# Norms of a two-block transformer kernel: sums of squares in token layout, root and reciprocal on 128 by 4, spread over partitions by products with the identity

## What is computed

```python
def rmsnorm(x, g, eps=1e-6):
    return x * rsqrt(mean(x * x, axis=-1, keepdims=True) + eps) * g

for layer in range(2):                                    # first block
    h = rmsnorm(x, g_attn) * (1 + scale1) + shift1        # norm 0, norm 2
    x = x + gate1 * mixer_layer(h, w_in, w_out, ...)
    h = rmsnorm(x, g_mlp) * (1 + scale2) + shift2         # norm 1, norm 3
    u, g = split(h @ w_up)
    x = x + gate2 * ((silu(conv(g)) * u) @ w_down)
x = rmsnorm(x, g_final)

h = rmsnorm(x, ln1)                                       # second block, norm 4
y_rnn, y_att = recurrent_group(h @ w_in), chunk_band_attention(h @ w_in)
mixed = concat([rmsnorm(y_rnn, gn_rnn), rmsnorm(y_att, gn_att)])    # the two group norms, 512 features each
x = x + mixed @ w_out
x = x + memory_cross_attention(rmsnorm(x, ln2), ...)
x = x + hierarchical_moe(rmsnorm(x, ln3), ...)
out = rmsnorm(x, final_norm)
```

## Time and profile before

| | us |
|---|---|
| median of 3 runs | 2549.05 (2545.45 to 2552.98) |
| the profiled execution | 2549.13 |
| its span in the trace | 2547.3 |
| PE busy | 2326.3 (91% of the span) |
| DVE busy | 1171.3 (46%) |
| ACT busy | 870.0 (34%) |

### The profile page before, as it was taken

The page is one execution under the profiler, slowest core; times in us unless marked ns, Lnnn a source line. Parts: engine busy times, 40 slices in busy tenths (PEclk is TensorE's granted clock), DMA queues, the critical chain, the costliest instruction groups (busy, mean ns, idle before and its releaser), DMA issues.

```text
span 2547.3 us, 33126 instructions
## 1 busy us (share of the span) xinstructions
PE 2326.3 (91%) x11912; PEld 1613.7 (63%) x11912; DVE 1171.3 (46%) x2263; ACT 870.0 (34%) x1607; POOL 80.9 (3%) x84
## 2 busy tenths in 40 slices
PE   5999989999998999989999999979989689888886
PEld 3777567888886775568888867847866333333332
DVE  4435755534535345646535435764442432323334
ACT  3323753322324224724313334463442121212222
POOL 0000000000000000000000000000000111111110
PEclk7999799999999996999999999989999799999998
DMA  8563035323332751033233222202413699999996
GB/s 267 173 183 108 1 110 156 96 78 107 93 90 72 207 167 38 2 100 83 100 91 99 91 84 67 91 26 66 149 50 148 231 396 399 410 408 403 411 391 264
DMA packets 251789, 414.43 MB, mean 163 GB/s; under 512 B 21447, under 2 KB 226897, under 8 KB 239185
## 3 DMA queue, kind: packets, MB, share of 16 engines
q1 hardware_dynamic: 235649, 398.25, 44.7%
q0 software_dynamic: 11520, 8.43, 1.0%
q10 hardware_dynamic: 4432, 5.24, 0.6%
HBM read 420.24 MB, written 25.17 MB: 175 GB/s over the span
## 4 chain that ended last, share of the span: by engine, by line
PE 77%; DMA 8%; DVE 7%; issue 4%; ACT 3%; SPq 1%; ACTq 0%; DVEq 0%; PEldq 0%; POOLq 0%; PEld 0%
PE bank L724 9%; PE bank L726 9%; PE bank L725 9%; DMA arena<-in_expert_up_w 7%; PE bank L652 6%; PE bank L654 6%; PE bank L653 6%; PE bank L1104 5%; PE bank L1105 3%; PE bank L1113 3%; PE bank L771 2%; PE bank L745 2%; PE bank L761 2%; PE bank L632 2%; PE bank L679 2%
## 5 line engine op out<-in xcount | busy, mean ns | idle before, releaser
L652 PE MATMUL bank<-hT_r,arena_r 128*128 128x512 f32 x704 | 296.1, 421 | 33.4 <-DVE arena_r L1667 21.2
L1104 PE MATMUL bank<-arena,xT 128*64 128x512 f32 x560 | 262.9, 626 | 49.8 <-DMA arena<-in_expert_up_w 35.9
L654 PE MATMUL bank<-hT_r,arena_r 128*128 128x512 f32 x704 | 278.1, 395 | 0.0
L726 PE MATMUL bank<-hT_r,arena_r 128*128 128x512 f32 x704 | 275.3, 391 | 0.0
L1105 PE MATMUL bank<-arena,xT 128*64 128x512 f32 x560 | 263.3, 627 | 0.0
L653 PE MATMUL bank<-arena_r 128*128 128x512 f32 x656 | 259.2, 395 | 0.0
L725 PE MATMUL bank<-arena_r,S_r 128*128 128x512 f32 x528 | 206.9, 392 | 0.0
L2224 DVE TENSOR_TENSOR hT<-hT,bank 64x512 f32<-64x512 f32 x80 | 54.8, 685 | 319.1 <-PE bank L1092 292.7
L1104 PEld LDWEIGHTS bank<-arena,xT 128*64 128x64 f32 x560 | 78.6, 144 | 166.7 <-issue 148.8
L652 PEld LDWEIGHTS bank<-hT_r,arena_r 128*128 128x128 f32 x704 | 134.5, 191 | 74.6 <-ACT hT_r L1239 22.0
L654 PEld LDWEIGHTS bank<-hT_r,arena_r 128*128 128x128 f32 x704 | 134.1, 191 | 29.3
(11 more groups left out here) (432 smaller groups left out, 4475.8 us busy)
## 6 DMA issues: line engine op xcount, KB each, us to landing
arena<-in_expert_gate_w SPq DMA_DIRECT2D x32, 2048.0 KB
arena<-in_expert_up_w SPq DMA_DIRECT2D x32, 2048.0 KB, 20.4
arena<-in_expert_down_w SPq DMA_DIRECT2D x32, 2048.0 KB, 14.0
arena<-in_w_up SPq DMA_DIRECT2D x88, 512.0 KB, 5.0
arena<-in_w_in SPq DMA_DIRECT2D x68, 512.0 KB, 6.1
arena<-in_w_down SPq DMA_DIRECT2D x40, 512.0 KB, 4.1
arena<-in_w_mod SPq DMA_DIRECT2D x16, 1024.0 KB, 10.0
S<-in_w_mod SPq DMA_DIRECT2D x32, 512.0 KB, 4.6
```

Source lines behind the costliest of these rows:

```text
L652: mm(b[:, :], w_h, hT_r[:, k, :], start=start, stop=False)
L654: return mm(b[:, :], w_l, hT_r[:, k, :], start=False, stop=stop)
L726: return mm(b[:, :], w_slot(arena_r, i, piece)[:, at:at + P], hi, start=False, stop=stop)
L1104: mm(bank[half][gate0:gate0 + SUB, :], x, expert_weights(slot, 0)[:, k, :], start=k == 0, stop=k == KD - 1)
```

## The change

The product is turned round: the tile of squares becomes the stationary operand, 128 tokens at a time, and a column of 1/1024 (or 1/512) the moving one, so that four products per tile of squares leave one mean per token, on 128 partitions by 4 columns. Root and reciprocal work on 128x4. A new step `spread` then makes the 128x512 table again: for each of the 4 columns the reciprocal root, broadcast along 128 columns, is the weight matrix, and the identity is the moving operand. DVE's gain products read the result straight from bank 7 (group norms: banks 4 and 5). It is done for norms 0 to 4 and the two group norms.

```diff
+        mean_of = sb("mean_of", [P, 2, NT])
+        norm_std, norm_root = small[:, 32:36], small[:, 36:40]
...
+            def token_sums(b, k, n, which):
+                for t in reversed(range(NT)):
+                    opens = k == 0 and t == NT - 1
+                    out, of = (bank[b][:, 0:NT], mean_of[:, which, :]) if opens else (bank[b][:, t:t + 1], mean_of[:, which, NT - 1:NT])
+                    ins = mm(out, sq[:, k % 2, t * P:(t + 1) * P], of, start=opens, stop=k == n - 1 and t == 0)
+                ins.then_inc(s["sq_used"], 1)
+
+            def spread(n, b):
+                pe.wait_ge(s["rs_ready"], n + 1)
+                for t in range(NT):
+                    ins = mm(bank[b][:, t * P:(t + 1) * P], norm_root[:, t:t + 1].to_broadcast([P, P]), ident, start=True, stop=True)
+                ins.then_inc(s["root_spread"], 1)
...
                 with pe.If(l > 0):
                     norm(2 * l, b=0)
+                spread(2 * l, 7)
...
                 norm(2 * l + 1, KD - 2)
+                spread(2 * l + 1, 7)
                 with pe.If(l < DEPTH - 1):
                     mod_next(l, MOD_FIRST - 1)
...
             norm(2 * L, b=0)
+            spread(2 * L, 7)
             pe.wait_ge(s["mem_scaled"], 2)
...
                 for k in range(CT):
                     pe.wait_ge(s["sq_ready"], 6 * KD + CT * grp + k + 1)
-                    mm(bank[7][:, :], onesR, sq[:, k % 2, :], start=k == 0, stop=k == CT - 1).then_inc(s["sq_used"], 1)
+                    token_sums(7, k, CT, 1)
+                spread(2 * L + 1 + grp, 4 + grp)
...
-                af(std[:, :], bank[7][:, :], ACT.Sqrt, bias=epsc[:, 0:1]).then_inc(s["std_ready"], 1)
+                af(norm_std, bank[7][:, 0:NT], ACT.Sqrt, bias=epsc[:, 0:1]).then_inc(s["std_ready"], 1)
...
+            def token_root(n, stds):
+                dve.wait_ge(s["std_ready"], stds)
+                vec.reciprocal(norm_root, norm_std).then_inc(s["rs_ready"], 1)
...
+                dve.wait_ge(s["root_spread"], n + 1)
-                        stt(hn[:, k % 2, :], xT[:, k, :], table[:, g + k:g + k + 1], rs[:, :], ALU.mult, ALU.mult).then_inc(s["hn_ready"], 1)
+                    stt(hn[:, k % 2, :], xT[:, k, :], pc[:, g + k:g + k + 1], bank[7][:, :], ALU.mult, ALU.mult).then_inc(s["hn_ready"], 1)
```

More of the change, by code:

```diff
@@ L139 @@
 FIN_AT = 13
-CH_NORM, CH_ROPE, CH_MLP = 1, 2, 2
+CH_ROPE, CH_MLP = 2, 2
 MLP_SLOTS = 2 * (UP_SLOTS + DOWN_SLOTS)
@@ L1221, in _, with norm_sum @@
             af(cz[:, :, 0:1].rearrange("p k o -> p (k o)"), small[:, 8:8 + KD], ACT.Silu).then_inc(s["silu_c"], 1)
-            def norm_sum(n, before, b=7, also=None):
+            def norm_sum(n, before, b=7, also=None, by_token=True):
                 for k in range(KD):
@@ L1232, in norm_sum @@
                 act.wait_ge(s["sq_used"], n * KD + KD)
-                af(std[:, :], bank[b][:, :], ACT.Sqrt, bias=epsc[:, 0:1]).then_inc(s["std_ready"], 1)
+                root, of = (norm_std, bank[b][:, 0:NT]) if by_token else (std[:, :], bank[b][:, :])
+                af(root, of, ACT.Sqrt, bias=epsc[:, 0:1]).then_inc(s["std_ready"], 1)
             def norm_shift(n, shift):
@@ L1326, in _ @@
             act.wait_ge(s["lam2_abs"], 1)
-            af(small[:, 40:44], small[:, 40:44], ACT.Exp, scale=-1.0).then_inc(s["lam2_exp"], 1)
+            af(small[:, 40:44], small[:, 40:44], ACT.Exp, scale=-1.0).then_inc(s["lam_exp"], 1)
             for c in range(MOD_FIRST):
@@ L1438, in _ @@
             act.wait_ge(s["sq_used"], 2 * L * KD + KD)
-            af(std[:, :], bank[0][:, :], ACT.Sqrt, bias=epsc[:, 2:3]).then_inc(s["std_ready"], 1)
+            af(norm_std, bank[0][:, 0:NT], ACT.Sqrt, bias=epsc[:, 2:3]).then_inc(s["std_ready"], 1)
             for k in range(KD):
@@ L1523, in beside_out2 @@
                     af(mem_hi[:, 2 * k - 2:2 * k, :], mem_full[:, 2 * k - 2:2 * k, :], ACT.Copy).then_inc(s["mem_ready"], 1)
-            norm_sum(7, 64, also=beside_out2)
+            norm_sum(7, 64, also=beside_out2, by_token=False)
             proj_split2(IN2 + OUT2 + 1)
@@ L1689, in _ @@
             vec.memset(one6[:, :], 1.0)
+            link(vec.memset(mean_of[:, :, :], 0.0))
+            for which, width in enumerate((D, D_RNN)):
+                vec.memset(mean_of[:, which, NT - 1:NT], 1.0 / width)
             vec.memset(gpad[:, :, :], 0.0)
@@ L1744, in norm_recip, with norm @@
                 link(vec.reciprocal(rs[:, :], std[:, :]))
-            def norm(n, g, table, shift, stds=None, out=hT, done="h_ready", halfway=False):
-                if not halfway:
-                    norm_recip(n if stds is None else stds)
+            def norm(n, g, shift):
+                dve.wait_ge(s["root_spread"], n + 1)
                 for k in range(KD):
[L1751 to L1754, removed]
-                        stt(hn[:, k % 2, :], xT[:, k, :], table[:, g + k:g + k + 1], rs[:, :], ALU.mult, ALU.mult).then_inc(s["hn_ready"], 1)
[L1756 to L1761, removed]
+                    if k >= 2:
+                        dve.wait_ge(s["h_ready"], n * KD + (k - 1))
+                        dve.wait_ge(s["h_lo_ready"], n * KD + (k - 1))
+                    stt(hn[:, k % 2, :], xT[:, k, :], pc[:, g + k:g + k + 1], bank[7][:, :], ALU.mult, ALU.mult).then_inc(s["hn_ready"], 1)
+                    if k >= 1:
+                        shift_rest(n, k - 1, shift)
+                shift_rest(n, KD - 1, shift)
             def shift_rest(n, k, shift):
@@ L1766, in shift_rest, with norm_split @@
                 stt(h_lo[:, k, :], hn[:, k % 2, :], pc[:, shift + k:shift + k + 1], hT_r[:, k, :], ALU.add, ALU.subtract).then_inc(s["h_lo_ready"], 1)
-            def norm_split(done, g, also=None):
+            def norm_split(done, g, root, also=None):
                 for k in range(KD):
@@ L1923, in _ @@
                         split_lo(l, 0)
-                norm(2 * l + 1, C_GM, pc, SH2)
+                token_root(2 * l + 1, 2 * l + 2)
+                norm(2 * l + 1, C_GM, SH2)
                 with dve.If(l < DEPTH - 1):
@@ L2030, in _ @@
             for grp, g in enumerate((E_GR, E_GA)):
-                dve.wait_ge(s["std_ready"], 7 + grp)
-                link(vec.reciprocal(rs[:, :], std[:, :]))
+                token_root(2 * L + 1 + grp, 7 + grp)
+                dve.wait_ge(s["root_spread"], 2 * L + 2 + grp)
                 src = (xc, o2)[grp]
```

39 lines of the change are left out of this document (20 added, 19 removed).

## The result

The changed kernel takes 2561.11 us (median of 8 runs, 2555.67 to 2566.83) against 2549.59 of the kernel before on the same chip (8 runs): a ratio of 1.0042, 95% interval 1.0032 to 1.0052, 11.5 us slower. Its profiled execution took 2561.64 us, with a span of 2559.8, 12.5 longer than before.

A forecast was written before the change was run, and what follows sets the result against it. PE's program was taken to bound the kernel (77% of the span). Terms 3.7 + 2.8 + 0 - 1.6 + 5.7 + 5.3 gave +15.9 us on the profiled 2549.13, so 2565 us, range 2543 to 2576.

The forecast's parts named there:

- Prices: Per operation: 64 records of sums 10.5 us (6.9 to 14.1), a spread 1.0 or 1.9, DVE's gain product unchanged.
- Rival 1: All new sums run at PE's upper clock level: -5.8 us, about -12 at best, time 2540; chance 0.17.
- Norm 0, +3.7: Sums and 48 modulation records end at 35.7 against 32.0, later work already at lower clock: 3.7 us slower.
- Norm 1, +2.8: Modulation chunk and folds now start behind the spread: first MLP product at 418.6, not 415.86, 2.8 us slower.
- Norm 2, 0: Sums of 10.5 us, then 2.55 to the gain product, at 795.25: no change (-4 to +4).
- Norm 3, -1.6: Three sums as before, then 2.55 us instead of 4.1 to the gain product: 1.6 us faster.
- Norm 4, +5.7: Transpositions wait behind the spread (+5.1) and later pairs cost more at the lower clock: 5.7 us slower.
- Group norms, +5.3: Second sums wait behind the first spread; 24 more projection products (5.4 us) follow the second norm: 5.3 us slower.

The follow-up runs named there:

- e5: Changed kernel with 128 moving columns instead of one in the sums, as many products and weight loads: 2540.75 us, 0.9971 of the kernel before.
- second trace: The changed kernel run once more, unedited, to trace it again: 2556.81 us, 1.0039 of the kernel before.
- e2: Changed kernel with only the order of work altered at norm 1, norm 4 and the group norms: 2553.61 us, 1.0016 of the kernel before.
- e3: Changed kernel with norm 4 and the two group norms back in the old form: 2546.60 us, 0.9994 of the kernel before.
- e7: Against e1, a dense product behind every tile instead of every second one at norms 2 and 4: 2560.27 us, 1.0047 of the kernel before.
- e1: Changed kernel plus an unread dense 512-column product behind every second tile of squares at norms 2 and 4: 2570.37 us, 1.0086 of the kernel before.

## Why the prediction was right, and where it wasn't

The direction, the mechanism at norms 2 and 4 and the range (2543 to 2576) held; 2565 was 4 us too high. Step by step:

- **Prices.** 64 records of sums were taken at 10.5 us: 10.29 and 10.73. The spread at 1.0 or 1.9: 1.16 or 2.08. The gain product with its operand in PSUM was taken at 0.75: two in 1.41. The run with the columns alone changed (e5) shows that the clock, and not the number of loads, made the difference between 7.6 and 10.3. Rival 1 put the kernel with all sums at the upper level at 2540; e5, which is that case, took 2540.75. That the two agree within 1 us is luck by 2 us, since the kernel before was 2547.58 in that series and not 2549.59; the rival's own sum, -5.8, stands against a measured -6.8. The Trainium skill ("TensorE: Matmul & The Clock Gate", section "LDWEIGHTS (loading the stationary operand)") gives a load of 128 columns 107 ns, with no term for the clock. Here 16 one-column records in 3.41 us at 0.50 are 213 ns each, and the loads' own records at norm 2 are 333 ns long on the mean at 0.50 against 192 at 1.00, so at the lower level the measurement decides against it.
- **Norm 0, +3.7.** This step failed. It rested on "What follows, folds and modulation products, is already at the lower level". In the first trace the 48 modulation records (256 columns each) ran in one piece behind the sums, the clock came back at 34, and the next six us ran at 0.97: the first projection product came 3.4 us sooner (1.1 of it was left at norm 1's root, 408.23 against 409.31). In the second trace it came 1.3 later than in the kernel before, and norm 1's root 3.5 later (412.78). In all seven traces with one-column sums at norm 0 the stretch 35 to 40 has a granted clock of 0.96 to 1.00, in both traces of the kernel before 0.50; so the premise was wrong each time, while the time itself went the forecast's way in two of the seven. What brings the clock back there no run shows.
- **Norm 1, +2.8.** 3.8 in three traces, 1.3 in two. In the three the chunk and the folds ran at the lower level from their first record or nearly so (6.99 us where 5.2 were taken), since the clock now falls at the end of the spread, which took 1.16 us itself; with wide sums ahead of it (e5) it doesn't fall there. The lost cover was as forecast.
- **Norm 2, 0:** -0.15. **Norm 3, -1.6:** -2.4, since the clock was still up behind the last sums and the spread took 1.16, not 1.9. **Norm 4, +5.7:** 6.2; e5 and e2 split it into clock (4.6 by e5) and order (1.7 to 2.3).
- **Group norms, +5.3:** 3.7. ACT's first high part came 3.35 us later against the sums' begin (3.3 forecast), the second reciprocal too (17.13 behind the first sum, 13.82 before). The mis-sized term is the last one, the 24 more projection products behind the second norm, 5.4. It priced all at 0.23, those of the kernel before too. But there the 24 products that stand behind the second norm began at the lower level:

```profile
1726.00:1732.00 6.00, 5.75 (x14) 0.51 0.00 0
```

  From 1726.25 to the first addition to x at 1734.02 the old kernel took 7.8 us for what I priced at 5.5. The changed one took 11.9 for its 48 (1731.51 to 1743.37), so the term was 4.1. The rows I had read end with the first of these products and don't show this.

The terms as measured (norm 0 between -3.4 and +1.3 at its own place) sum to +7.7 to +12.4; the forecast's +15.9 was too high by norm 0 and the group norms, and too low by 1.0 at norm 1 and 0.5 at norm 4. So its closeness is partly luck: the total came no lower than 4 us below it because norms 1 and 4 cost more than forecast and some 3 us appeared where no term stood.

What stays open: 3 us of the traces' 12.5 appear between the output projection of the second block and the end (the lag is 9.35 at its first addition, 1743.37 against 1734.02). No experiment placed them. And e2's total moved by 3.3 us more than its places do, e3's by 4.6 more than norm 4 and the group norms had cost, of which the upper level behind its group norms is 2.4.

## What to carry to other kernels

A product that is turned round to make a step on another engine cheap must be priced at the clock that it leaves behind, for itself and for what follows: 32 one-column products (64 records) cost 10.3 us, 32 with 128 columns 7.6, with the same loads. If weight loads set the pace anyway, as they did here, try a moving operand with more columns, up to what the loads hide. And work that lay beside a slow operation needs a new place before that operation is made fast: at norm 4 the old reciprocal had not been on the chain, and the spread that its replacement needs, standing ahead of the transpositions, cost about 2 us.

## What the runs showed of the hardware

- Columns that nobody needs were almost free beside weight loads: 16 records with one column took 1.95 us at norm 1, with 128 columns (e5) 2.05, both at clock 1.00.
- The clock fell with PE busy without a gap. The Trainium skill ("TensorE: Matmul & The Clock Gate", section "HAM oscillation — how this bites in real kernels") tells of falls through idle gaps while PE waits for data. The stretch 788 to 791 of the changed kernel, busy 3.00 of 3.00 us at 0.62, is a fall of another kind.
- Dense products mixed in held the clock in e7 and not in e1, where they only became twice as dear.
- With the same program the clock fell at 24 us in one execution and at 22 in another, and the first projection product moved by 4.7 us with it. One trace of such a place is not enough to size a term; here not even its sign is the same in all.
